# A transformer layer in fp32 by split matmuls: signs of two weight sums turned, two sums made in one VectorE operation, and a third made by an adding transfer that GpSimd issues

## Chip, cores, metric

The kernel runs on one core of a Trainium2 chip. The metric is device microseconds of one execution, as the median of several runs. Lower is better.

## The reference, cut to what matters

One layer of a hybrid decoder on 256 tokens of width 2048, all in float32:

```
xn   = rms_norm(h);  proj = xn @ w_in          # DeltaNet heads and attention heads
h    = h + concat(o_gdn, o_moba) @ w_o
hn   = rms_norm(h)
h    = h + (silu(hn @ w_gate) * (hn @ w_up)) @ w_down      # inner width 5632
gate = sigmoid(rms_norm(h) @ w_ple_gate)
h    = h + gate * (p @ w_ple_proj)
```

The change is in the last three lines: in the products with `w_gate` and `w_up`, with `w_down`, and with `w_ple_gate`.

## The kernel before

**Units.** A unit is 256 rows by 512 columns of a weight, held as `raw[j]`, 128 partitions x 2 x 512 float32 (512 KB). SyncE's queue (SP) loads it with one transfer into a ring of four buffers. ScalarE rounds it (`w_hi`), VectorE takes the remainder (`w_lo`, in `split`), and TensorE computes each product in three matmuls of 512 columns: hi by hi, hi by lo, lo by hi. A plain unit costs TensorE 12 matmuls. ScalarE and VectorE work three units ahead of TensorE (`LEAD = 3`). The load of unit u waits until `split` of unit u-4 is done (`lo_ready`), since it takes that buffer. ScalarE's rounding of unit u waits until TensorE has used unit u-4.

**Mixed units.** For some pairs of units the 2x2 block product is formed from seven products in place of eight (Winograd's form of Strassen), 21 matmuls for two units in place of 24. In a gate/up block of 16 units the pairs are (4, 5), (7, 8) and (10, 11) (`MIXED`, `SEQ`); the first block has its own order `FIRST_SEQ`, with pairs (5, 6), (8, 9) and (11, 12). There are 11 such blocks: 6 and 5, each group followed by a `down` stage of two halves with two pairs per half. The stage of the last gate (`PG_SEQ`) has pairs (6, 7) and (11, 12). That makes 43 pairs. In a pair, g is the first unit and u the second, each with two rows of 512 columns, 0 and 1. VectorE makes four weight sums in `split_mixed`:

```
t3 = u1 - u0          (L1913)
t1 = u0 - g0          (L1915, written over u0 in raw)
t2 = u1 - t1          (L1917)
t4 = g1 - t2          (L1919)
```

Then it splits unit u (whose first row is now t1), lets ScalarE round t3 alone (L1447) and t2 and t4 together (L1451), and takes the remainders t_lo (L1924 for t3, L1926 for t2 and t4). ScalarE rounds unit u (L1444) after t1 is there. TensorE (`mixed_units`) uses g, then u, then t3, then t2 and t4.

**What follows the sums.** SP's load four units after g waits for t4 (`t4_ready`), because t4 reads g's buffer; all later loads stand behind it in SP's order. In a loop block the load of unit 8 waits so for the sums of pair (4, 5), and that of unit 11 for the sums of pair (7, 8). In each loop block ScalarE and VectorE also turn the last block's activations between the parts of the first pair (`turned`, L1437 and L1903).

**GpSimd** makes masks at the start and small powers during the first half. In the stretch of the change it had two tasks, each of two tiny operations (`rstd`, L565 and L567): the inverse root of the mean square of h, once in the first gate/up block and once before the last gate.

Of the kernel before, what the change touches and what calls it, by code (L numbers as in the profile page):

```python
# [30 lines left out]
P = 128  # L31
# [182 lines left out]
def build(nc, A):  # L214
    FIRST, AT, BANK_OF = plan()

    with ExitStack() as ctx:
# [37 lines left out]
        for c in range(2):  # L255
# [40 lines left out]
        t3_raw = sb("t3_raw", [P, CB], at=mix + 62 * KIB)  # L296
# [15 lines left out]
        t24_raw = sb("t24_raw", [P, 2, CB], at=triu_at)  # L312
# [8 lines left out]
        assert triu_at + 4 * KIB <= place[0]  # L321
        rows = sb("rows", [NROW - KT, P])
        gains = sb("gains", [P, NROW + 2])
        G_ATTN, G_FFN, G_PLE, G_GDN, G_Q, G_K = 0, KT, 2 * KT, 3 * KT, 3 * KT + 1, 3 * KT + 2
        G_QS, G_OG = NROW, NROW + 1
# [4 lines left out]
        sc = {n: sb(n, [P, NT, HEADS]) for n in ("beta", "dt_in", "dt_abs", "dt_exp", "dt_ln", "dt_sum", "g", "gc", "egc")}  # L330
        ba_s = sb("ba_s", [P, NT, 2 * HEADS])
        ba_parts = sb("ba_parts", [P, NT, 4 * HEADS])
        warm = sb("warm", [P, 1])
# [54 lines left out]
        t1_ready, t2_ready, t3_ready, t4_ready = (sem(f"t{n}_ready") for n in (1, 2, 3, 4))  # L388
        t3_hi_ready, t24_hi_ready, t3_lo_ready, t24_lo_ready, t_used = (
            sem(n) for n in ("t3_hi_ready", "t24_hi_ready", "t3_lo_ready", "t24_lo_ready", "t_used"))  # L390
# [68 lines left out]
        def _(sp):  # L459
# [42 lines left out]
            for u0, u1, n, at, mg, md in ((U_GUA, U_DA, FF_A, 0, MIX_GUA, MIX_DA), (U_GUB, U_DB, FF_B, FF_A, MIX_GUB, MIX_DB)):  # L502
                def gate_up(i, seq):

                    for j, (side, g) in enumerate(seq):
                        w = w_gate if side == "gate" else w_up
                        if j >= RING and seq[j - RING] in [("gate", m) for m in MIXED]:
                            sp.wait_ge(t4_ready, i * len(MIXED) + (mg + MIXED.index(seq[j - RING][1]) + 1))
                            fetch(j, w, KU * g, i * CB + at * CB)
                        else:  # L510
                            load(i * (2 * UPB) + (u0 + j), j, w, KU * g, i * CB + at * CB)

                gate_up(0, SEQ if at else FIRST_SEQ)
                with sp.Fori(1, n) as i:
                    gate_up(i, SEQ)
                seq, dm, _ = down_order(n)
                with sp.Fori(0, 2) as i:
                    for j, (side, g) in enumerate(seq):
                        k, col = at * 4 + KU * g, i * (2 * CB) + side * CB
                        if j >= RING and seq[j - RING] in [(0, m) for m in dm]:  # L520
                            sp.wait_ge(t4_ready, i * 2 + (md + dm.index(seq[j - RING][1]) + 1))
                            fetch(j, w_down, k, col)
                        else:
                            load(i * len(seq) + (u1 + j), j, w_down, k, col)
            for b in range(4):
                load(U_PP + b, b, w_pp, 0, b * CB)
            for j, (side, g) in enumerate(PG_SEQ):
                if j >= RING and PG_SEQ[j - RING] in [(0, m) for m in PG_MIXED]:
                    sp.wait_ge(t4_ready, MIX_PG + PG_MIXED.index(PG_SEQ[j - RING][1]) + 1)
# [15 lines left out]
        def _(pool):  # L545
# [91 lines left out]
            for i in range(2):  # L637
                pool.wait_ge(h_sum, i + 1)
                rstd(h_rs[i][:], h_ms[i][:], h_s[i][:], 1.0 / D, EPS, h_rstd, i)


        @block.tensor
        def _(pe):
# [295 lines left out]
            def mixed_units(u, j, q, n):  # L939

                first, last = q == 0, q == len(MIXED) - 1
                g, a0, a1 = MIXED[q], slice(0, P), slice(P, TOK)
                k0, k1 = KU * g, KU * g + 1
                gh, gl = w_hi[j % RING], w_lo[j % RING]
                uh, ul = w_hi[(j + 1) % RING], w_lo[(j + 1) % RING]
                use(u)
                product(bg[0][:], xT_hi[:, k0, a0], xT_lo[:, k0, a0], gh[:, 0, :], gl[:, 0, :], first, last)
                product(pair[0][0][:], xT_hi[:, k1, a0], xT_lo[:, k1, a0], gh[:, 1, :], gl[:, 1, :], False,
                        last).then_inc(unit_used, 1)
                use(u + 1)  # L950
# [3 lines left out]
                pe.wait_ge(t3_lo_ready, n)  # L954
                product(bg[2][:], F_hi[:, q, 2, :], F_lo[:, q, 2, :], t_hi[:, 2, :], t_lo[:, 2, :], first, last)
                pe.wait_ge(t24_lo_ready, n)
                product(bg[1][:], F_hi[:, q, 0, :], F_lo[:, q, 0, :], t_hi[:, 0, :], t_lo[:, 0, :], first, last)
                product(pair[0][1][:], xT_hi[:, k1, a1], xT_lo[:, k1, a1], t_hi[:, 1, :], t_lo[:, 1, :], False,
                        last).then_inc(t_used, 1)
# [48 lines left out]
            def down(ud, bd, n, n0, m0, turn_last):  # L1008
# [3 lines left out]
                for m in range(2):  # L1012
                    c = m + (2 if n0 else 0)
                    for j, (side, g) in enumerate(seq):
# [7 lines left out]
                        if g in dm:  # L1022
# [25 lines left out]
                            pe.wait_ge(t3_lo_ready, count)  # L1048
                            product(bg[2][:], D_hi[:, q, 2, :], D_lo[:, q, 2, :], t_hi[:, 2, :], t_lo[:, 2, :], first, last)
                            pe.wait_ge(t24_lo_ready, count)  # L1050
                            product(bg[1][:], D_hi[:, q, 0, :], D_lo[:, q, 0, :], t_hi[:, 0, :], t_lo[:, 0, :], first, last)
                            product(pair[0][1][:], actT_hi[:, k1, a1], actT_lo[:, k1, a1], t_hi[:, 1, :], t_lo[:, 1, :], False,
# [32 lines left out]
            for j, (side, g) in enumerate(PG_SEQ):  # L1085
# [4 lines left out]
                if g in PG_MIXED:  # L1090
# [18 lines left out]
                    pe.wait_ge(t3_lo_ready, MIX_PG + q + 1)  # L1109
                    product(bg[2][:], E_hi[:, q, 3, :], E_lo[:, q, 3, :], t_hi[:, 2, :], t_lo[:, 2, :], first, last)  # L1110
                    pe.wait_ge(t24_lo_ready, MIX_PG + q + 1)
                    product(bg[1][:], E_hi[:, q, 1, :], E_lo[:, q, 1, :], t_hi[:, 0, :], t_lo[:, 0, :], first, last)
                    product(pair[0][1][:], xT_hi[:, k1, a1], xT_lo[:, k1, a1], t_hi[:, 1, :], t_lo[:, 1, :], False,
# [38 lines left out]
        def _(act):  # L1152
# [424 lines left out]
        def _(dve):  # L1577
# [328 lines left out]
            def split_mixed(u, j, n, first, between):  # L1906
# [45 lines left out]
            def add(o, a, b, done, count=None):  # L1952
# [3 lines left out]
                v.tensor_tensor(o, a, b, ALU.add).then_inc(done, 1)  # L1956

            def down(ud, n, n0, m0):

                seq, dm, end = down_order(n)  # L1960
                for j in range(2 * len(seq)):
# [15 lines left out]
                    if jj == end:  # L1977
# [3 lines left out]
                        add(v_s[:], bg[1][:], v_s[:], down_sum)  # L1981
                        add(u_s[:], bg[2][:], v_s[:], down_sum, d0 + 2)
                    if jj == end + 1:
                        add(o10, o10, u_s[:], down_sum, d0 + 3)
# [11 lines left out]
            def gate_up(i, u0, b0, n0, peeled, m0):  # L1996
                seq = FIRST_SEQ if peeled and n0 == 0 else SEQ
                mixed_end = seq.index(("up", MIXED[-1]))
                for j in range(2 * UPB):
# [15 lines left out]
                    if j == mixed_end:  # L2015
                        p1 = act_s[1]
                        dve.wait_ge(p1_copied, i + (n0 + (2 if n0 else 0) + 1))
                        v.tensor_tensor(v_s[:], bg[1][:], p1[:], ALU.add).then_inc(v_ready, 1)
# [4 lines left out]
                        v.tensor_tensor(gate_s[1][:], pair[0][1][:], u_s[:], ALU.add).then_inc(gate_sum, 1)  # L2023
# [29 lines left out]
            for u in range(U_PP, UNITS):  # L2053
# [12 lines left out]
                if u == U_PG + PG_END:  # L2066
                    dve.wait_ge(p1_copied, done + 4 + 1)
                    v.tensor_tensor(v_s[:], bg[1][:], act_s[1][:], ALU.add).then_inc(v_ready, 1)
# [4 lines left out]
                    v.tensor_tensor(gate_s[1][:], pair[0][1][:], u_s[:], ALU.add).then_inc(gate_sum, 1)  # L2073
# [36 lines left out]
```

## Time and profile before

| | |
|---|---|
| time, median of 3 runs | 1308.66 us (1308.38 to 1309.03) |
| span of the profiled execution | 1306.8 us |
| profiled execution's own time beside its span | not listed apart; the median is 1.9 us above the span |
| TensorE busy | 1299.9 us of the span |
| VectorE busy | 1041.3 us |
| ScalarE busy | 710.7 us |
| GpSimd busy | 57.2 us |
| read from HBM | 235.36 MB |

The span runs from the first to the last instruction. Matmuls are pipelined, so one that shows as 0.39 us long starts 0.23 us after the one before it. Idle time of an engine other than the one that sets the pace costs nothing by itself.

### The profile page before, as it was taken

The page shows a single profiled execution, that of the slowest core. Times are in us where ns is not written, and L with a number is a line of the kernel's source. Part 1 is how long each engine was busy: PE and PEld are TensorE (multiplying, and loading weights), DVE is VectorE, ACT ScalarE, POOL GpSimd, SP SyncE. Part 2 cuts the span into 40 slices and gives each one's busy share as a digit, 9 for nine tenths or more (in the row PEclk, how much of TensorE's full clock was granted, in tenths as well). Part 3 has the DMA queues.
Part 4 walks back from the last instruction along what each step waited for, and adds up shares of the span by engine and source line. Part 5 has one row for each costly group of instructions (what it writes and reads, how often), then busy time and mean ns, then how long its engine had stood idle before and what let it go on. Part 6 is the DMA issues. An engine that isn't in the chain of part 4 may idle for free.

```text
span 1306.8 us, 18407 instructions
## 1 busy us (share of the span) xinstructions
PE 1299.9 (99%) x6589; PEld 1074.1 (82%) x6589; DVE 1041.3 (80%) x1409; ACT 710.7 (54%) x946; POOL 57.2 (4%) x71
## 2 busy tenths in 40 slices
PE   9999999999999999999999999999999999999998
PEld 8788888888888888888888888888888888888887
DVE  6578885788586668999888978679888987968784
ACT  6576444544455556655555654445555555555653
POOL 5003000221000000000000000000000000000000
PEclk9999999999999999999999999999999999999999
DMA  8555554455444555665566656566666566556554
GB/s 272 178 176 162 160 147 129 146 147 148 145 127 145 178 176 161 215 219 181 188 198 205 204 187 215 182 211 188 195 205 214 181 189 210 190 178 224 178 179 163
DMA packets 126204, 238.37 MB, mean 182 GB/s; under 512 B 9711, under 2 KB 10786, under 8 KB 126138
## 3 DMA queue, kind: packets, MB, share of 16 engines
q1 hardware_dynamic: 126106, 237.48, 58.2%
q8 instruction: 42, 0.69, 0.2%
q14 instruction: 24, 0.20, 0.0%
q10 hardware_dynamic: 32, 0.01, 0.0%
HBM read 235.36 MB, written 2.10 MB: 182 GB/s over the span
## 4 chain that ended last, share of the span: by engine, by line
PE 97%; DVE 2%; ACT 0%; DMA 0%; issue 0%; DVEq 0%; ACTq 0%
PE pair L654 15%; PE pair L656 15%; PE pair L655 15%; PE pair L935 12%; PE pair L937 12%; PE pair L936 12%; PE bg L935 2%; PE bg L936 2%; PE bg L937 2%; PE bg L775 2%; PE bg L845 2%; PE bg L712 1%; PE bg L930 1%; DVE w_lo L1583 1%; PE bg L826 0%; PE bg L687 0%
## 5 line engine op out<-in xcount | busy, mean ns | idle before, releaser
L1583 DVE TENSOR_TENSOR w_lo<-raw,w_hi 128x1024 fp32r<-128x1024 f32 x442 | 533.1, 1222 | 160.7 <-ACT w_hi L1163 158.8
L1163 ACT ACTIVATE w_hi<-raw 128x1024 fp32r<-128x1024 f32 x399 | 416.4, 1056 | 254.6 <-PE pair L656 117.0
L654 PE MATMUL pair<-w_hi,xT_hi 128*128 128x512 f32 x716 | 289.7, 405 | 0.0
L656 PE MATMUL pair<-w_hi,xT_lo 128*128 128x512 f32 x716 | 279.9, 391 | 0.0
L655 PE MATMUL pair<-w_lo,xT_hi 128*128 128x512 f32 x716 | 279.4, 390 | 0.0
L656 PEld LDWEIGHTS pair<-w_hi,xT_lo 128*128 128x128 f32 x716 | 134.5, 188 | 29.1
L654 PEld LDWEIGHTS pair<-w_hi,xT_hi 128*128 128x128 f32 x716 | 134.7, 188 | 26.7 <-DVE w_lo L1583 0.3
L655 PEld LDWEIGHTS pair<-w_lo,xT_hi 128*128 128x128 f32 x716 | 134.9, 188 | 24.7
L1444 ACT ACTIVATE w_hi<-raw 128x1024 fp32r<-128x1024 f32 x43 | 45.7, 1063 | 141.5 <-DVE raw L1915 140.0
L935 PE MATMUL pair<-w_hi,actT_hi 128*128 128x512 f32 x296 | 115.7, 391 | 0.0
L937 PE MATMUL pair<-w_hi,actT_lo 128*128 128x512 f32 x296 | 115.2, 389 | 0.0
L936 PE MATMUL pair<-w_lo,actT_hi 128*128 128x512 f32 x296 | 115.2, 389 | 0.0
L935 PE MATMUL pair<-w_hi,xT_hi 128*128 128x512 f32 x226 | 88.2, 390 | 0.9 <-DVE w_lo L1583 0.9
L936 PE MATMUL pair<-w_lo,xT_hi 128*128 128x512 f32 x226 | 87.9, 389 | 0.0
L937 PE MATMUL pair<-w_hi,xT_lo 128*128 128x512 f32 x226 | 87.9, 389 | 0.0
L937 PEld LDWEIGHTS pair<-w_hi,actT_lo 128*128 128x128 f32 x296 | 55.6, 188 | 11.6
L936 PEld LDWEIGHTS pair<-w_lo,actT_hi 128*128 128x128 f32 x296 | 55.6, 188 | 11.4
L935 PEld LDWEIGHTS pair<-w_hi,actT_hi 128*128 128x128 f32 x296 | 55.6, 188 | 11.3
L1926 DVE TENSOR_TENSOR t_lo<-t_raw,t_hi 128x1024 fp32r<-128x1024 f32 x43 | 52.4, 1218 | 0.0
L935 PEld LDWEIGHTS pair<-w_hi,xT_hi 128*128 128x128 f32 x226 | 42.4, 188 | 10.5 <-DVE w_lo L1583 1.8
L937 PEld LDWEIGHTS pair<-w_hi,xT_lo 128*128 128x128 f32 x226 | 42.4, 188 | 8.9
L936 PEld LDWEIGHTS pair<-w_lo,xT_hi 128*128 128x128 f32 x226 | 42.4, 188 | 8.7
(386 smaller groups left out, 1959.8 us busy)
## 6 DMA issues: line engine op xcount, KB each, us to landing
raw<-in_w_in_dram SPq DMA_DIRECT2D x112, 512.0 KB, 3.8
raw<-in_w_gate_dram SPq DMA_DIRECT2D x88, 512.0 KB, 4.4
raw<-in_w_up_dram SPq DMA_DIRECT2D x88, 512.0 KB, 4.4
raw<-in_w_down_dram SPq DMA_DIRECT2D x88, 512.0 KB, 4.8
raw<-in_w_o_dram SPq DMA_DIRECT2D x32, 512.0 KB, 4.4
raw<-in_w_ple_gate_dram SPq DMA_DIRECT2D x32, 512.0 KB, 4.8
raw<-in_w_ple_proj_dram SPq DMA_DIRECT2D x4, 512.0 KB, 4.3
h<-in_x_dram SPq DMA_DIRECT2D x3, 512.0 KB, 7.8
```

Of the source, the lines that this page charges most:

```text
L654: mm(banks[t][:], hi[:, ts], wh, start=first, stop=False)
L655: mm(banks[t][:], hi[:, ts], wl, start=False, stop=False)
L656: m = mm(banks[t][:], lo[:, ts], wh, start=False, stop=last)
L775: m = mm(out[r][rs, j, :], lhs, rhs, start=True, stop=True)
L845: last = mm(o, l, r, start=True, stop=True)
L935: mm(o, hi, wh, start=first, stop=False)
L936: mm(o, hi, wl, start=False, stop=False)
L937: return mm(o, lo, wh, start=False, stop=last)
L1163: f(w_hi[j % RING][:], raw[j % RING][:], ACT.Copy).then_inc(hi_ready, 1)
L1444: f(w_hi[j % RING][:], raw[j % RING][:], ACT.Copy).then_inc(hi_ready, 1)
L1583: v.tensor_tensor(w_lo[j % RING][:], raw[j % RING][:], w_hi[j % RING][:].bitcast(F32), ALU.subtract).then_inc(lo_ready, 1)
L1926: v.tensor_tensor(t_lo[:, 0:2, :], t24_raw[:], t_hi[:, 0:2, :].bitcast(F32), ALU.subtract).then_inc(t24_lo_ready, 1)
```

## The change

The sums of g enter with the other sign, so that what was subtracted is added and the results are subtracted where they were added:

```
t1 = u0 + g0                       (made by a transfer)
t2 = u1 - t1
t3, t4 = g + t2                    (one operation on 128 x 1024: g0 + t2 and g1 + t2)
```

The first sum is made by a transfer from GpSimd's queue that reads g's first row (128 x 512, 256 KB) and adds it to u's first row in place. GpSimd waits until both units have landed, then issues it; ScalarE's rounding of u and VectorE's t2 wait for its 16 completion counts. The three sums lie side by side in `t_raw`; they are rounded by one ScalarE operation and their remainders taken by one VectorE operation of 128 x 1536. TensorE waits once for all three. GpSimd's 43 transfers stand in program order with its two `rstd` tasks: the first task stands between the second and the third transfer of the first block, the second task ahead of both transfers of the last gate. In the loop blocks, ScalarE's part of `turned` now stands ahead of its rounding of the sums. No instruction of TensorE is added or removed.

```
-                v.tensor_tensor(t3_raw[:], raw[ju][:, 1, :], raw[ju][:, 0, :], ALU.subtract).then_inc(t3_ready, 1)
-                dve.wait_ge(t3_ready, n)
-                v.tensor_tensor(raw[ju][:, 0, :], raw[ju][:, 0, :], raw[jg][:, 0, :], ALU.subtract).then_inc(t1_ready, 1)
-                dve.wait_ge(t1_ready, n)
-                v.tensor_tensor(t24_raw[:, 0, :], raw[ju][:, 1, :], raw[ju][:, 0, :], ALU.subtract).then_inc(t2_ready, 1)
+                dve.wait_ge(t1_ready, n * 16)
+                v.tensor_tensor(t_raw[:, 0, :], raw[ju][:, 1, :], raw[ju][:, 0, :], ALU.subtract).then_inc(t2_ready, 1)
                 dve.wait_ge(t2_ready, n)
-                v.tensor_tensor(t24_raw[:, 1, :], raw[jg][:, 1, :], t24_raw[:, 0, :], ALU.subtract).then_inc(t4_ready, 1)
+                v.tensor_tensor(t_raw[:, 1:3, :], raw[jg][:], t_raw[:, 0:1, :].to_broadcast([P, 2, CB]),
+                                ALU.add).then_inc(t34_ready, 1)
                 split(u, j)
                 if between:
                     between()
-                dve.wait_ge(t3_hi_ready, n)
-                v.tensor_tensor(t_lo[:, 2, :], t3_raw[:], t_hi[:, 2, :].bitcast(F32), ALU.subtract).then_inc(t3_lo_ready, 1)
-                dve.wait_ge(t24_hi_ready, n)
-                v.tensor_tensor(t_lo[:, 0:2, :], t24_raw[:], t_hi[:, 0:2, :].bitcast(F32),
-                                ALU.subtract).then_inc(t24_lo_ready, 1)
+                dve.wait_ge(t_hi_ready, n)
+                v.tensor_tensor(t_lo[:], t_raw[:], t_hi[:].bitcast(F32), ALU.subtract).then_inc(t_lo_ready, 1)
...
+            def first_sum(u, j, n):
+                jg, ju = (j - 1) % RING, j % RING
+                pool.wait_ge(raw_landed[jg], (u - 1 - jg) * (16 // RING) + 16)
+                pool.wait_ge(raw_landed[ju], (u - ju) * (16 // RING) + 16)
+                g.dma_start(raw[ju][:, 0, :], raw[jg][:, 0, :], accum_op=ALU.add).then_inc(t1_ready, 16)
...
+                    first_sum(i * (2 * UPB) + (u0 + j), j, i * len(MIXED) + (m0 + q + 1))
+                    if normed and q == 1:
+                        norm(0)
...
+            norm(1)
+            for q, m in enumerate(PG_MIXED):
+                j = PG_SEQ.index((1, m))
+                first_sum(U_PG + j, j, MIX_PG + q + 1)
...
-                act.wait_ge(t1_ready, n)
+                act.wait_ge(t1_ready, n * 16)
                 act.wait_ge(unit_used, u - (RING - 1))
                 f(w_hi[j % RING][:], raw[j % RING][:], ACT.Copy).then_inc(hi_ready, 1)
+                if between:
+                    between()
                 if not n0_first:
                     act.wait_ge(t_used, n - 1)
-                f(t_hi[:, 2, :], t3_raw[:], ACT.Copy).then_inc(t3_hi_ready, 1)
-                if between:
-                    between()
-                act.wait_ge(t4_ready, n)
-                f(t_hi[:, 0:2, :], t24_raw[:], ACT.Copy).then_inc(t24_hi_ready, 1)
+                act.wait_ge(t34_ready, n)
+                f(t_hi[:], t_raw[:], ACT.Copy).then_inc(t_hi_ready, 1)
```

SP's waits on `t4_ready` become waits on `t34_ready`, with the same counts. The results' signs are turned back in operations that were there before, by `subtract` in place of `add`.

## Rows read from the trace of the kernel before

**Rows 1.** The page: busy time by engine.
```profile
PE 1299.9 (99%) x6589; PEld 1074.1 (82%) x6589; DVE 1041.3 (80%) x1409; ACT 710.7 (54%) x946; POOL 57.2 (4%) x71
```

**Rows 2.** The page: the chain that ended last, shares by engine.
```profile
PE 97%; DVE 2%; ACT 0%; DMA 0%; issue 0%; DVEq 0%; ACTq 0%
```

**Rows 3.** Busy time by stretch: PE, PEld, DVE, ACT, POOL, clock, DMA share, GB/s.
```profile
600.00:700.00 100.00, 100.00 (x451) 82.96 (x450) 92.54 (x109) 56.45 (x65) 0.00 (x0) 1.00 0.63 197
```

**Rows 4.** First block, TensorE and VectorE: start, duration, instruction, idle before it.
```profile
522.90 0.50 PE L935 MATMUL pair<-w_hi,xT_hi 128*128 128x512 f32 x1 [0.61 <-DVE w_lo L1583]
...
531.02 0.50 PE L935 MATMUL pair<-w_hi,xT_hi 128*128 128x512 f32 x1 [0.30 <-DVE w_lo L1583]
...
532.51 0.39 PE L935 MATMUL bg<-t_hi,F_hi 128*128 128x512 f32 x1
...
518.84 0.69 DVE L1913 TENSOR_TENSOR t_raw<-raw 128x512 f32<-128x512 f32 x1
```

**Rows 5.** Groups by line: count, busy us, mean ns, idle before.
```profile
L1915 DVE TENSOR_TENSOR raw<-raw,raw 128x512 f32<-128x512 f32 x43 | 29.8, 692 | 1.5
...
L1926 DVE TENSOR_TENSOR t_lo<-t_raw,t_hi 128x1024 fp32r<-128x1024 f32 x43 | 52.4, 1218 | 0.0
...
L1451 ACT ACTIVATE t_hi<-t_raw 128x1024 fp32r<-128x1024 f32 x43 | 45.1, 1048 | 0.0
```

**Rows 6.** One loop block, VectorE and ScalarE in order of time.
```profile
633.42 0.69 DVE L1913 TENSOR_TENSOR t_raw<-raw 128x512 f32<-128x512 f32 x1
...
642.76 0.69 DVE L1913 TENSOR_TENSOR t_raw<-raw 128x512 f32<-128x512 f32 x1
...
650.81 0.69 DVE L1913 TENSOR_TENSOR t_raw<-raw 128x512 f32<-128x512 f32 x1
...
636.43 1.09 ACT L1437 ACTIVATE actT_hi<-bg 128x512 f32 x2
```

**Rows 7.** The same block, loads of units 5, 8, 11: issue, time to landing.
```profile
L468 SPq DMA_DIRECT2D raw<-in_w_up_dram x1: 373/373/373, 624.6 to 624.6; - x1
...
DMA to landing us min/median/max: 4.6/4.6/4.6
...
L468 SPq DMA_DIRECT2D raw<-in_w_up_dram x1: 373/373/373, 636.3 to 636.3; - x1
...
DMA to landing us min/median/max: 3.5/3.5/3.5
...
L468 SPq DMA_DIRECT2D raw<-in_w_up_dram x1: 372/372/372, 645.7 to 645.7; - x1
...
DMA to landing us min/median/max: 3.6/3.6/3.6
```

**Rows 8.** The same block, TensorE: first use of t_lo, pairs two and three.
```profile
649.49 0.39 PE L935 MATMUL bg<-t_hi,F_hi 128*128 128x512 f32 x1
...
656.97 0.39 PE L935 MATMUL bg<-t_hi,F_hi 128*128 128x512 f32 x1
```

**Rows 9.** Transfers by kind: KB each, us to landing.
```profile
out_dram<-h SPq DMA_DIRECT2D x1, 256.0 KB, 2.4
```

**Rows 10.** GpSimd's two small tasks in order of time.
```profile
524.75 1.09 POOL L565 TENSOR_SCALAR h_ms<-h_s 128x2 f32<-128x2 f32 x1 [137.64 <-DVE h_s L2014]
525.92 1.55 POOL L567 TENSOR_TENSOR h_rs<-h_ms,half 128x2 f32<-128x2 f32 x1
...
1228.00 0.62 POOL L565 TENSOR_SCALAR h_ms<-h_s 128x2 f32<-128x2 f32 x1 [700.52 <-DVE h_s L2064]
1228.70 1.15 POOL L567 TENSOR_TENSOR h_rs<-h_ms,half 128x2 f32<-128x2 f32 x1
```

**Rows 11.** Last gate, TensorE's first use of t_lo, pairs one and two.
```profile
1235.27 0.39 PE L935 MATMUL bg<-t_hi,E_hi 128*128 128x512 f32 x1
...
1248.19 0.39 PE L935 MATMUL bg<-t_hi,E_hi 128*128 128x512 f32 x1
```

**Rows 12.** Last gate, the load of unit 12, issued at 1234.8: time to landing.
```profile
DMA to landing us min/median/max: 5.2/5.2/5.2
```

More of the change, by code:

```diff
@@ L311, in build @@
         triu_at = place[0]
[L312 removed]
+        t_raw = sb("t_raw", [P, 3, CB], at=triu_at)
         triu = sb("triu", [P, P])
@@ L329, in build @@
         exp_a = sb("exp_a", [P, HEADS])
-        sc = {n: sb(n, [P, NT, HEADS]) for n in ("beta", "dt_in", "dt_abs", "dt_exp", "dt_ln", "dt_sum", "g", "gc", "egc")}
         ba_s = sb("ba_s", [P, NT, 2 * HEADS])
         ba_parts = sb("ba_parts", [P, NT, 4 * HEADS])
+        assert triu_at + 6 * KIB <= place[0]
+        gains = sb("gains", [P, NROW + 2])
+        G_ATTN, G_FFN, G_PLE, G_GDN, G_Q, G_K = 0, KT, 2 * KT, 3 * KT, 3 * KT + 1, 3 * KT + 2
+        G_QS, G_OG = NROW, NROW + 1
+        sc = {n: sb(n, [P, NT, HEADS]) for n in ("beta", "dt_in", "dt_abs", "dt_exp", "dt_ln", "dt_sum", "g", "gc", "egc")}
         warm = sb("warm", [P, 1])
@@ L636, in _, with norm, gate_up @@
                         post(*s)
-            for i in range(2):
+            def norm(i):
                 pool.wait_ge(h_sum, i + 1)
                 rstd(h_rs[i][:], h_ms[i][:], h_s[i][:], 1.0 / D, EPS, h_rstd, i)
+            def first_sum(u, j, n):
[3 more added lines that the diff above has]
+                g.dma_start(raw[ju][:, 0, :], raw[jg][:, 0, :], accum_op=ALU.add).then_inc(t1_ready, 16)
+            def gate_up(i, u0, m0, seq, normed):
+                for q, m in enumerate(MIXED):
+                    j = seq.index(("up", m))
+                    first_sum(i * (2 * UPB) + (u0 + j), j, i * len(MIXED) + (m0 + q + 1))
+                    if normed and q == 1:
+                        norm(0)
+            for n, n0, ug, ud, mg, md in ((FF_A, 0, U_GUA, U_DA, MIX_GUA, MIX_DA), (FF_B, FF_A, U_GUB, U_DB, MIX_GUB, MIX_DB)):
+                for i in range(n):
+                    gate_up(i, ug, mg, SEQ if n0 or i else FIRST_SEQ, not (n0 or i))
+                seq, dm, _ = down_order(n)
+                for m in range(2):
+                    for q, k in enumerate(dm):
+                        j = m * len(seq) + seq.index((1, k))
+                        first_sum(ud + j, j, md + 2 * m + q + 1)
+            norm(1)
+            for q, m in enumerate(PG_MIXED):
+                j = PG_SEQ.index((1, m))
+                first_sum(U_PG + j, j, MIX_PG + q + 1)
         @block.tensor
@@ L953, in mixed_units @@
                         False).then_inc(unit_used, 1)
-                pe.wait_ge(t3_lo_ready, n)
-                product(bg[2][:], F_hi[:, q, 2, :], F_lo[:, q, 2, :], t_hi[:, 2, :], t_lo[:, 2, :], first, last)
-                pe.wait_ge(t24_lo_ready, n)
+                pe.wait_ge(t_lo_ready, n)
+                product(bg[2][:], F_hi[:, q, 2, :], F_lo[:, q, 2, :], t_hi[:, 1, :], t_lo[:, 1, :], first, last)
                 product(bg[1][:], F_hi[:, q, 0, :], F_lo[:, q, 0, :], t_hi[:, 0, :], t_lo[:, 0, :], first, last)
-                product(pair[0][1][:], xT_hi[:, k1, a1], xT_lo[:, k1, a1], t_hi[:, 1, :], t_lo[:, 1, :], False,
+                product(pair[0][1][:], xT_hi[:, k1, a1], xT_lo[:, k1, a1], t_hi[:, 2, :], t_lo[:, 2, :], False,
                         last).then_inc(t_used, 1)
@@ L1108, in _ @@
                             False).then_inc(unit_used, 1)
-                    pe.wait_ge(t3_lo_ready, MIX_PG + q + 1)
-                    product(bg[2][:], E_hi[:, q, 3, :], E_lo[:, q, 3, :], t_hi[:, 2, :], t_lo[:, 2, :], first, last)
-                    pe.wait_ge(t24_lo_ready, MIX_PG + q + 1)
+                    pe.wait_ge(t_lo_ready, MIX_PG + q + 1)
+                    product(bg[2][:], E_hi[:, q, 3, :], E_lo[:, q, 3, :], t_hi[:, 1, :], t_lo[:, 1, :], first, last)
                     product(bg[1][:], E_hi[:, q, 1, :], E_lo[:, q, 1, :], t_hi[:, 0, :], t_lo[:, 0, :], first, last)
-                    product(pair[0][1][:], xT_hi[:, k1, a1], xT_lo[:, k1, a1], t_hi[:, 1, :], t_lo[:, 1, :], False,
+                    product(pair[0][1][:], xT_hi[:, k1, a1], xT_lo[:, k1, a1], t_hi[:, 2, :], t_lo[:, 2, :], False,
                             last).then_inc(t_used, 1)
@@ L1950, in turned_forms, with add @@
                                 ALU.subtract).then_inc(ff_free[q], 1)
-            def add(o, a, b, done, count=None):
+            def add(o, a, b, done, count=None, op=ALU.add):
                 if count:
                     dve.wait_ge(down_sum, count)
-                v.tensor_tensor(o, a, b, ALU.add).then_inc(done, 1)
+                v.tensor_tensor(o, a, b, op).then_inc(done, 1)
             def down(ud, n, n0, m0):
@@ L2022, in gate_up @@
                         dve.wait_ge(v_ready, i * 2 + (2 * n0 + 2))
-                        v.tensor_tensor(gate_s[1][:], pair[0][1][:], u_s[:], ALU.add).then_inc(gate_sum, 1)
+                        v.tensor_tensor(gate_s[1][:], pair[0][1][:], u_s[:], ALU.subtract).then_inc(gate_sum, 1)
                     if j == 2 * UPB - 1:
@@ L2067, in _ @@
                     dve.wait_ge(p1_copied, done + 4 + 1)
-                    v.tensor_tensor(v_s[:], bg[1][:], act_s[1][:], ALU.add).then_inc(v_ready, 1)
+                    v.tensor_tensor(v_s[:], bg[1][:], act_s[1][:], ALU.subtract).then_inc(v_ready, 1)
                     v.tensor_tensor(gate_s[0][:], pair[0][0][:], act_s[1][:], ALU.add).then_inc(gate_sum, 1)
@@ L2072, in _ @@
                     dve.wait_ge(v_ready, 2 * done + 2)
-                    v.tensor_tensor(gate_s[1][:], pair[0][1][:], u_s[:], ALU.add).then_inc(gate_sum, 1)
+                    v.tensor_tensor(gate_s[1][:], pair[0][1][:], u_s[:], ALU.subtract).then_inc(gate_sum, 1)
                     v.tensor_tensor(v_s[:], bg[3][:], v_s[:], ALU.add).then_inc(pg_parts, 1)
```

29 lines of the change are left out of this document (11 added, 18 removed).

## The prediction, made before the changed kernel was run

> **What bounds the kernel now.** I read the page's busy times first: TensorE is busy for 1299.9 of 1306.8 us, VectorE for 1041.3 [rows 1]. Then the chain that ended last: 97% of it is TensorE, 2% VectorE [rows 2]. So a shorter VectorE can give back only what TensorE loses to it. The places where it does are in the first gate/up block, where two matmuls waited for a remainder [rows 4]. In step, matmuls start 0.23 us apart; the one at 522.90 was due at 522.13 and the one at 531.02 at 530.56. That is 0.77 + 0.46 = 1.23 us, and it is all that the change can gain there. The table by stretch says what to fear instead: in the loop blocks VectorE is busy 92.5 of 100 us while TensorE has no gap [rows 3]. The two run close together, so a new delay ahead of VectorE may reach TensorE.
>
> **The change part by part.**
>
> *VectorE.* Per pair the four sums (4 x 0.69) and two remainders become one sum of 512 columns, one of 1024 and one remainder of 1536 [rows 5]. A 1024 operation takes 1.22, so 512 more columns add 0.53: the remainder of 1536 takes 1.75. VectorE saves about 1.0 us per pair, 43 us in all. Outside the first block this work is hidden behind TensorE, so I put its worth at nothing beyond the 1.23 us.
>
> *ScalarE.* One rounding of 1536 columns, about 1.5 us (1.05 for 1024, half as much again [rows 5]), starts only when both sums of the second operation are there. From the start of t2 the new order of a pair is: t2 and the double sum ready at +2.0 (0.73 from start to start, 1.22, a signal), rounding until +3.5, remainder until +5.3. Before, the last remainder ended at about +5.7 from the start of t3 (from 650.81) [rows 5, 6], which was VectorE's first sum.
>
> *The transfer, S.* From the landing of unit u to the moment when ScalarE and VectorE may go on, there is now one transfer of 256 KB within SBUF that reads two sources. No such operation is in the trace. From below, a plain store of 256 KB late in the kernel, from SP's queue, took 2.4 us from issue to landing [rows 9]; the sum reads the destination as well, is issued by GpSimd, whose smallest operations take 0.6 to 1.5 us [rows 10], and shares engines that are 63% busy [rows 3]. From above, the slowest load shown, twice the bytes and beside others, took 5.2 [rows 12]. I take S = 4.0: 2.4, plus 1.0 for GpSimd, plus 0.6 for the second read and the sharing; it is an estimate from these rows, between the two bounds.
>
> By the Trainium skill (DMA: Bandwidth & Descriptors, Anatomy of one DMA) a transfer issued from GpSimd takes about 2.0 us plus its bytes at 436 GB/s, which gives an estimate of 2.6 us for 256 KB; with it the total below would be 1314.3. The rows show no transfer from GpSimd, so the trace neither agrees nor differs; that case is the quick rival below.
>
> *One loop block with S = 4.0.* Pair (4, 5): unit 5's load is issued at 624.6 and lands after 4.6 [rows 7], its sum at 633.2; VectorE comes to the pair at 633.4 [rows 6], so no wait. The double sum is ready at 635.4 and SP issues the load of unit 8, 0.9 us earlier than before (636.3). ScalarE now first turns the activations, at 636.43 to 637.5 [rows 6], and rounds the three sums until 639.05; the remainder ends at 640.8, two splits follow (2.3), and VectorE is free for the second pair at 643.1, no earlier than before (642.76). Unit 8 lands 3.5 after issue, at 638.9; its sum at 642.9. Still no wait. The double sum is ready at 645.1, unit 11 lands 3.6 later at 648.7 [rows 7], and its sum is there at 652.7. VectorE would be free at 643.1 + 7.6 = 650.7 (5.2 for the pair, 2.3 for two splits), so here it waits 2.0. The remainder ends at 652.7 + 5.3 = 658.0. TensorE first uses it at 656.97 [rows 8]: it stalls 1.0 us. The second pair's remainder, at 648.4, is in time (649.49). TensorE sets the pace of the block, so the stall is not won back.
> As a rule: S - 2.95 per block from S = 2.95 to 4.2. Above 4.2 the first two pairs are late too, three transfers stand in one chain, and the stall is 3S - 11.4. With 10 blocks (the first of the second group has the same order): 10.5 us.
>
> *The down stages.* Their pairs lie four units apart with no turning between them; one hop has more cover. I put them at nothing up to S = 4; late, they would cost 2S - 7.7 twice by the same steps, 0.3 us each at 4.0 and 2.3 at 5.0. Small; left out of the sum.
>
> *The first block.* GpSimd's first small task now stands ahead of the third sum. It takes 2.7 us (524.75 to 527.47 [rows 10]) and starts when VectorE has done the second pair. VectorE came to that pair at 518.84 [rows 4] and will at about 518.4; its remainder ends 5.3 later, the mean square goes out at 523.8, the task ends at 526.6, the third sum lands at 526.6 + S, its remainder 5.3 later at 535.9. TensorE used it at 532.51 [rows 4], without the two waits at 531.28. Stall 4.6, less the 1.23 won: S - 0.6 = 3.4 us net.
>
> *The last gate.* The second small task stands ahead of the first sum there. It ends at 1229.85 [rows 10], though unit 7 has long landed. First sum at 1233.9, remainder at 1239.2, where TensorE wants it at 1235.27 [rows 11]: stall S - 0.07. The second pair: its load waits for the split after the first pair, at 1229.9 + S + 6.4, lands after 5.2 [rows 12], taken as 5.0; the sum takes S again, the remainder 5.3. That ends at 1246.6 + 2S = 1254.6 against 1248.19 [rows 11]. Stall in all 2S - 1.6 = 6.4 us. VectorE's cover does not help, for here the transfers wait for GpSimd and for the load.
>
> *Sum.* 10.5 + 3.4 + 6.4 = 20.3 us on the span of 1306.8: 1327.1. The median stood 1.9 above the span, so 1329.
>
> **Rivals.**
> *A quick transfer, S below 3.* The loop blocks have no stall, and the two fixed places remain: at 2.4, 1.8 + 3.2 = 5.0, time 1313.7. For it speaks the store of 2.4 us [rows 9]; against it, that this is a store with nothing else moving, from a queue other than GpSimd's.
> *Not slower.* GpSimd's small tasks lose their effect if S is 1.6 or less: then the last gate costs 1.6 and the first block 1.0, in all 2.6, about what can be told from no change; time 1311. At 1.0 it is 0.9 + 0.4 = 1.3 us, time 1310. It is decided by the one number S at the place of the second task. Against it: below every transfer of the rows. Faster by over 0.2% would take more than the 1.23 us that VectorE costs TensorE now.
> *A slow transfer, S of 5 or more.* Three transfers and two loads stand in one chain in each loop block: at 5.0 the blocks cost 36, the down stages 4.6, the first block 4.4, the last gate 8.4, together 53, time 1362. For it: VectorE is busy 92.5% [rows 3], and GpSimd's two operations took 1.09 and 1.55 in the first task but 0.62 and 1.15 in the second [rows 10], as if something held them; each pair's transfer also runs beside a load issued 1.1 us after the pair's own.
> The Trainium skill warns of this (SBUF — State Buffer, Who interferes with whom): GpSimd's writing of descriptors is blocked while VectorE runs an operation that holds both port pairs, but a sum of two SBUF tensors takes only the read side, so by the page this kernel's VectorE would not delay the transfer, and the time would be the first sum's; no row before shows which.
>
> **How the numbers follow.** S from 3 to 4.6, the forecast: 0.52. Quick, 1.7 to 3: 0.20, slower by a little. Slow, above 4.6: 0.18. Not slower: 0.10, of which 0.05 faster for gains that I don't see. With S at 1.9, under the store's 2.4, the two fixed places cost 3.5 and the time is 1312; at 5.0 it is 1362. The range 1311 to 1362 leaves out some 2 in 10. A measurement here tells about 0.2%, 2.6 us, from no change. Faster 0.05; the same 0.11 (the rest of that rival and part of the quick one); slower 0.84.
>
> **What would show it.** In the profile after, the 43 transfers should land about 4 us after issue. TensorE's waits should stand at the third pair of each loop block, about 1 us each, at the third pair of the first block and at both pairs of the last gate, all released by VectorE's t_lo or by the split, and VectorE before them by the transfer. VectorE's busy time should fall by about 43 us to 998, ScalarE's by about 7. If TensorE waits nowhere in the loop blocks, S was under 3. If it also runs through the last gate, the small task was not in the way. If waits stand at the second pair already, S was over 4.2. The prediction is wrong if S is outside 3 to 4.6, or if the loads become slower beside the transfers.

## The result and the profile after

The change made the kernel slower: 1399.09 us median (1396.62 to 1402.63) against 1308.76 measured beside it, a ratio of 1.069 [1.0676, 1.0708]. The forecast was 1329, the range 1311 to 1362. The profiled execution spans 1400.9 us, 94.1 more than before.

First the page after, busy time by engine and the chain that ended last, against [rows 1, 2].

```profile
PE 1332.5 (95%) x6589; PEld 1086.2 (78%) x6589; DVE 1005.3 (72%) x1280; ACT 708.7 (51%) x903; POOL 93.1 (7%) x114
...
PE 63%; DMA 18%; DVE 11%; ACT 4%; issue 3%; POOL 0%; DVEq 0%; ACTq 0%; POOLq 0%; SPq 0%
```

VectorE lost 36 us of busy time and TensorE, with the same 6589 matmuls, gained 32.6. TensorE's idle time, span less busy, went from 6.9 to 68.4. So 94.1 = 61.5 of idle time + 32.6 of longer busy time: two amounts to explain, not one. The chain, 97% TensorE before, now is 63% TensorE and 18% DMA.

TensorE's waits in the kernel after: who waited for whom, us in total, times, longest (`pair` and `bg` are what its matmuls write).

```profile
PE pair L962 <- DVE w_lo L1606: 36.2, 13, 3.8
PE bg L962 <- DVE w_lo L1606: 16.9, 8, 3.7
PE bg L962 <- DVE t_lo L1945: 5.7, 11, 0.6
PE bg L962 <- DVE actT_lo L1926: 2.7, 1, 2.7
```

VectorE is named, but VectorE itself waited. The groups of the kernel after say for what (count, busy us, mean ns, idle before and its releaser); the last row is GpSimd's transfer.

```profile
L1468 ACT ACTIVATE w_hi<-raw 128x1024 fp32r<-128x1024 f32 x43 | 45.6, 1060 | 185.4 <-DMA raw<-raw 179.1
...
L1937 DVE TENSOR_TENSOR t_raw<-raw 128x512 f32<-128x512 f32 x43 | 29.8, 692 | 114.3 <-DMA raw<-raw 112.2
L645 POOL DMA_DIRECT2D raw<-raw x43 | 37.2, 866 | 843.8 <-DMA raw<-in_w_up_dram 590.0
```

One loop block shows how: its three transfers, and the load of unit 13 (duration of the issue in ns, when; then time to landing).

```profile
L645 POOL DMA_DIRECT2D raw<-raw x3: 859/859/862, 649.1 to 668.9; - x3
...
DMA to landing us min/median/max: 3.4/3.6/7.0
...
L466 SPq DMA_DIRECT2D raw<-in_w_up_dram x1: 372/372/372, 669.1 to 669.1; - x1
...
DMA to landing us min/median/max: 7.0/7.0/7.0
```

The first two transfers took 3.6 and 3.4. The third, issued at 668.88 with a load 0.25 behind it, took 7.0, and so did that load. The same block in order of time: VectorE's second sum, then TensorE.

```profile
675.90 0.69 DVE L1937 TENSOR_TENSOR t_raw<-raw 128x512 f32<-128x512 f32 x1 [5.66 <-DMA raw<-raw]
...
674.83 0.39 PE L964 MATMUL pair<-w_hi,xT_lo 128*128 128x512 f32 x1
679.04 0.79 PE L962 MATMUL pair<-w_hi,xT_hi 128*128 128x512 f32 x1 [3.83 <-DVE w_lo L1606]
679.63 0.63 PE L963 MATMUL pair<-w_lo,xT_hi 128*128 128x512 f32 x1
```

After the wait matmuls are 0.42 to 0.6 us apart instead of 0.23. The table by stretch tells why (PE busy with matmuls, granted clock, DMA share, GB/s).

```profile
670.00:675.00 5.00, 5.00 (x24) 1.00 0.73 156
675.00:679.00 4.00, 0.21 (x1) 0.96 0.06 6
679.00:680.00 1.00, 0.96 (x2) 0.50 0.76 176
680.00:681.00 1.00, 1.00 (x4) 0.50 0.95 358
681.00:682.00 1.00, 1.00 (x4) 0.50 0.91 295
682.00:683.00 1.00, 1.00 (x5) 0.97 0.48 182
683.00:685.00 2.00, 2.00 (x11) 1.00 0.69 170
```

TensorE was idle from 675.2 to 679.0; for the next 3 us the granted clock was 0.50, the lower of its two levels (1.2 GHz). Of the 17 waits of over 2 us in the stretch of the change 14 were followed by such a stretch at 0.50, none of the shorter ones was by itself. In five of the 14 it began before the wait ended, by up to 1.2 us. The last row of the same table over all 14 stretches:

```profile
sum 54.59, PE 50.74; mean PE 3.62
```

TensorE was busy for 50.7 us at 0.50, and at half the rate some 25 of them are loss, 1.8 us for each of the 14. Most of the other 7 us are no slower work: a matmul shows as 0.39 us long but the next one starts after 0.23, so the first 0.16 of a wait counts as busy, 5.3 us for the 33 waits of the lines above.

Over all 43 transfers the split is sharp. Nineteen had a load issued between 1.0 us before and 0.55 after them; they took 5.3 to 7.0 us, median 6.2. Twenty-four had none: 3.2 to 4.3, median 3.4. The third pair of every loop block is of the first kind, and so are six of the eight of the down stages.

### The profile page after: what moved, and what is told of

The parts are those of the page before. It is cut to its first block, busy times and chain, and to the rows that moved or that the text cites. A ratio compares the mean times of both kernels' runs of the same rounds, so it can differ in the third digit from the quotient of the medians.

```text
span 1400.9 us, 18364 instructions
## 1 busy us (share of the span) xinstructions
PE 1332.5 (95%) x6589; PEld 1086.2 (78%) x6589; DVE 1005.3 (72%) x1280; ACT 708.7 (51%) x903; POOL 93.1 (7%) x114
## 4 chain that ended last, share of the span: by engine, by line
PE 63%; DMA 18%; DVE 11%; ACT 4%; issue 3%; POOL 0%; DVEq 0%; ACTq 0%; POOLq 0%; SPq 0%
PE pair L681 12%; PE pair L683 11%; PE pair L682 11%; DMA raw<-raw 10%; PE pair L962 6%; PE pair L963 6%; PE pair L964 6%; DMA raw<-in_w_up_dram 5%; DVE w_lo L1606 4%; DVE t_raw L1939 3%; ACT t_hi L1474 2%; DMA raw<-in_w_down_dram 2%; DVE t_raw L1937 2%; PE bg L802 2%; PE bg L872 1%
## 5 line engine op out<-in xcount | busy, mean ns | idle before, releaser
L683 PEld LDWEIGHTS pair<-w_hi,xT_lo 128*128 128x128 f32 x716 | 134.4, 188 | 29.1
L682 PEld LDWEIGHTS pair<-w_lo,xT_hi 128*128 128x128 f32 x716 | 134.8, 188 | 24.7
L1937 DVE TENSOR_TENSOR t_raw<-raw 128x512 f32<-128x512 f32 x43 | 29.8, 692 | 114.3 <-DMA raw<-raw 112.2
L645 POOL DMA_DIRECT2D raw<-raw x43 | 37.2, 866 | 843.8 <-DMA raw<-in_w_up_dram 590.0
L1945 DVE TENSOR_TENSOR t_lo<-t_raw,t_hi 128x1536 fp32r<-128x1536 f32 x43 | 75.6, 1758 | 19.6 <-ACT t_hi L1474 19.6
L1474 ACT ACTIVATE t_hi<-t_raw 128x1536 fp32r<-128x1536 f32 x43 | 63.9, 1487 | 38.7 <-DVE t_raw L1939 38.7
```

The source lines that it names most:

```text
L682: mm(banks[t][:], hi[:, ts], wl, start=False, stop=False)
L683: m = mm(banks[t][:], lo[:, ts], wh, start=False, stop=last)
L1474: f(t_hi[:], t_raw[:], ACT.Copy).then_inc(t_hi_ready, 1)
L1937: v.tensor_tensor(t_raw[:, 0, :], raw[ju][:, 1, :], raw[ju][:, 0, :], ALU.subtract).then_inc(t2_ready, 1)
L1945: v.tensor_tensor(t_lo[:], t_raw[:], t_hi[:].bitcast(F32), ALU.subtract).then_inc(t_lo_ready, 1)
```

## Experiments

The first four were to decide between three theories. **A**: the loss is the wait for the transfer, 3.5 us alone and 6 to 7 beside a load, with slow matmuls behind it. **B**: the transfers' traffic slows TensorE's weight loads. **C**: one wait for three sums, with the turning of the activations ahead of their rounding, makes the remainders late.

**e1: VectorE makes the first sum, no transfer.** All else as in the kernel after.

```
-  g.dma_start(raw[ju][:, 0, :], raw[jg][:, 0, :], accum_op=ALU.add).then_inc(t1_ready, 16)
...
+  v.tensor_tensor(raw[ju][:, 0, :], raw[ju][:, 0, :], raw[jg][:, 0, :], ALU.add).then_inc(t1_ready, 1)
```

> The changed kernel with the first sum made by VectorE again (added, 128 x 512) and no transfer from GpSimd; the turned signs, the double sum, the one rounding and the one remainder stay. Theory A (the loss is the wait for the transfer): 1306 to 1309 us, at most the 1.23 us that VectorE cost TensorE before are won. Theory B (the transfers' traffic slows the weight loads): the same, since the traffic is gone. Theory C (one wait for all three sums, and turning the activations ahead of their rounding, makes the remainders late): 1330 us or more, TensorE waiting for t_lo in each loop block.

1317.15 us, ratio 1.0063 [1.0049, 1.0076]. So 82 of the 90 us go with the transfer; 8.4 stay, which A did not expect and C had far too large. In nine of the ten loop blocks TensorE now waits 0.39 to 0.43 for the third pair's remainder, in the first block three times 0.6 and in a down stage once 0.5. One such place of e1, VectorE's remainder and TensorE's wait for it:

```profile
659.02 1.76 DVE L1921 TENSOR_TENSOR t_lo<-t_raw,t_hi 128x1536 fp32r<-128x1536 f32 x1 [0.48 <-ACT t_hi L1449]
...
660.84 0.50 PE L937 MATMUL bg<-t_hi,F_hi 128*128 128x512 f32 x1 [0.43 <-DVE t_lo L1921]
```

**e2: e1 with 43 transfers that nobody waits for** (192 KB each, a buffer added onto itself, at the places of the real ones).

```
+  g.dma_start(idle_b[:], idle_b[:], accum_op=ALU.add).then_inc(idle_done, 16)
```

> As the kernel before this one, with VectorE's own first sum, and beside it GpSimd issues 43 adding transfers at the same points, of 192 KB within a buffer that nothing reads. Theory A: within 3 us of the kernel without them, 1306 to 1312 us; the transfers themselves land after 3 to 7 us. Theory B: 1350 us or more, weight loads landing later by over 1 us. Theory C: as the kernel without them.

1317.17 us, ratio 1.0067 [1.0051, 1.0082]: e1's time, though these transfers took 2.9 to 6.4 us themselves. The loads of gate, up and down weights landed after 4.1, 4.4 and 4.7 us in the median, against 4.0, 4.4 and 4.6 in e1. B falls: the traffic, here three quarters of the bytes, costs nothing that shows; the waiting does.

**e3: the load of unit 13 held in the loop blocks until the third sum has landed and VectorE has used it.**

```
+  elif seq is SEQ and j == 13:
+      sp.wait_ge(t2_ready, i * len(MIXED) + (mg + 3))
+      fetch(j, w, KU * g, i * CB + at * CB)
```

> The changed kernel, but in the ten gate/up blocks after the first SP issues the load of unit 13 only when VectorE has made t2 of the third pair (some 4 us later), so that no load starts beside the third transfer. Theory A (a transfer takes 3.5 us alone and 6 to 7 beside a load that starts with it): the third transfers fall from 5.8 to 7.0 us to about 3.5, TensorE's waits at the third pair from 2.5 to 3.8 us to under 1, and with the slow matmuls behind them 4 us per block are won: 1350 to 1365 us. Theory B or a slowness of the third transfer for another reason (its buffers, GpSimd): transfers stay at 6 us and the time within 10 us of 1399, or longer, since a load was put off.

1360.36 us, ratio 1.039 [1.0374, 1.0406]: 38.7 less than the kernel after for a load that starts later. The third transfers of the loop blocks fell to 3.3 to 3.8, here that of the block shown above:

```profile
L648 POOL DMA_DIRECT2D raw<-raw x1: 862/862/862, 659.9 to 659.9; - x1
...
DMA to landing us min/median/max: 3.3/3.3/3.3
```

The waits for w_lo behind them are gone in seven of the ten blocks and at most 0.9 in the others, and one of 0.6 for t_lo stands in each. That is A.

**e4: GpSimd's two small tasks behind the sums that they preceded.**

```
-  if normed and q == 1:                 # first block
+  if normed and q == 2:
...
-  norm(1)                               # last gate: ahead of both sums
...
+  if q == 0:                            # behind the first sum
+      norm(1)
```

> The changed kernel with GpSimd's two small tasks put behind the transfer that they stood ahead of (the first behind the third sum of the first block, the second behind the first sum of the last gate). If they delayed these sums, as the prediction had it: the first block wins 2 to 4 us, the last gate 2 to 3 us, time 1393 to 1396. If they were not in the way: 1399 within 2 us.

1378.62 us, ratio 1.0539 [1.0509, 1.0568]: 20 less, where I expected 3 to 6. Most of the gain is in the loop blocks, which the edit does not touch: there the load now came 0.48 to 0.62 us after the third transfer instead of 0.25 to 0.45, and the median of these transfers fell from 6.3 to 4.7. What moved the two apart by some 0.2 us was not settled. It led to e9.

**e5 and e6: which half of C.** Both start from e1. In e5 ScalarE turns the activations behind its rounding, as the kernel before did:

```
-  if between:
-      between()
...
   act.wait_ge(t34_ready, n)
   f(t_hi[:], t_raw[:], ACT.Copy).then_inc(t_hi_ready, 1)
+  if between:
+      between()
```

> The kernel after without its transfer (VectorE makes the first sum), and ScalarE turns the activations behind its rounding of the three sums again instead of ahead of it. The kernel with the first sum on VectorE took 1317.2, 8.4 over the kernel before, with a wait of TensorE of 0.4 us for the remainder of the third pair in each loop block. Theory T (the turning, about 1.1 us once in a block ahead of the first pair's rounding, delays a VectorE that works without a break up to the third pair): the wait goes, and the time is within 2 us of the kernel before, 1307 to 1311. Rival R (the one rounding of 1536 columns ends 0.4 to 0.5 later than VectorE is ready for it, in every pair): the wait stays in the loop blocks, 1314 to 1317.

In e6 the second sum is rounded as soon as it is there:

```
+  act.wait_ge(t2_ready, n)
+  f(t_hi[:, 0, :], t_raw[:, 0, :], ACT.Copy)
   act.wait_ge(t34_ready, n)
-  f(t_hi[:], t_raw[:], ACT.Copy).then_inc(t_hi_ready, 1)
+  f(t_hi[:, 1:3, :], t_raw[:, 1:3, :], ACT.Copy).then_inc(t_hi_ready, 1)
```

> The kernel after without its transfer (VectorE makes the first sum), and ScalarE rounds the second sum as soon as it is there and the third and fourth by an operation of 1024 columns, so that the last rounding ends some 0.4 us earlier; the turning stays ahead of it. Theory R (the late rounding): VectorE's waits of 0.48 us for the rounding go in every pair, TensorE's waits in the loop blocks with them, 1308 to 1312. Theory T (the turning): little changes, 1315 to 1318. If both count: between, 1311 to 1315.

e5 took 1322.65 us, ratio 1.0106 [1.0091, 1.0122], slower than e1 by 5.5: the turned activations come late now, and the wait for t_lo stays. Two rows of e5, one block:

```profile
600.60 0.49 PE L937 MATMUL bg<-w_hi,xT_hi 128*128 128x512 f32 x1 [0.40 <-DVE actT_lo L1901]
...
618.91 0.50 PE L937 MATMUL bg<-t_hi,F_hi 128*128 128x512 f32 x1 [0.32 <-DVE t_lo L1921]
```

e6 took 1309.19 us, ratio 1.0002 [0.9993, 1.0011]: the kernel before again, with TensorE busy as before:

```profile
PE 1300.9 (99%) x6589; PEld 1074.2 (82%) x6589; DVE 1035.5 (79%) x1323; ACT 714.7 (55%) x946; POOL 56.4 (4%) x71
```

So the whole 8 us was the one rounding of 1536 columns, which ends 0.48 after VectorE is ready for it. From the first sum's start to the remainder's end VectorE takes 5.75 us for a pair in the kernel before, 6.05 in e1 and 5.57 in e6 (medians of 43). The turned signs, the double sum, the one remainder and the turning ahead of the rounding together cost nothing and bring nothing.

**e7: ten extra matmuls ahead of the wait in the third pair** (into a bank that is free then; their result is not used).

```
+  for _ in range(fill if q == 2 else 0):
+      mm(bg[3][:], xT_hi[:, 0, a0], xT_hi[:, 0:2, :].rearrange("p k n -> p (k n)"), start=True, stop=True)
   use(u + 1)
...
+  mixed_units(u, j, q, i * len(MIXED) + (m0 + q + 1), 0 if peeled else 10)
```

> The kernel after with ten extra matmuls of 512 columns (2.3 us, their result is not used) ahead of TensorE's wait in the third pair of the eight loop blocks that are not the first of their group. Theory: TensorE stood idle there for 2.5 to 3.8 us, and the granted clock then was 0.50 for 3 us, in which it did half of its work; with the idle time mostly filled the clock stays at 1.00, and each block gains about 1.5 us, 1399 - 12 = 1387 (1383 to 1391). Rival (the matmuls after the wait are slow because their operands come late or because the transfers take memory bandwidth): the same 1397 to 1403, or later by what the extra matmuls add where a wait is shorter than 2.3.

1392.57 us, ratio 1.0634 [1.0618, 1.065], some 6.5 less with 90 matmuls more (they stand in nine blocks, not in the eight that I counted). The profiled executions tell more. 90 x 0.227 = 20.4 us of matmuls were added; TensorE's busy time without them is 1343.5 - 20.4 = 1323.1, 9.4 less than after, and idle time with them is 48.4 + 20.4 = 68.8, as after. So the wait is the same and the matmuls behind it are faster. The same place of the block in e7:

```profile
675.00:676.00 1.00, 1.00 (x6) 1.00 0.00 0
676.00:677.00 1.00, 0.68 (x3) 1.00 0.33 39
677.00:678.00 1.00, 1.00 (x6) 1.00 0.77 240
```

The clock stays at 1.00, here and in all nine filled blocks; in the kernel after it had fallen in seven of them. The gain, 1.0 us per block, is two thirds of what I expected; a shorter wait of 0.57 for t_lo came up in most of these blocks, which had been hidden behind the slow matmuls.

**e8: half the columns, 128 KB** (half of the first sum is left out).

```
-  g.dma_start(raw[ju][:, 0, :], raw[jg][:, 0, :], accum_op=ALU.add).then_inc(t1_ready, 16)
+  g.dma_start(raw[ju][:, 0, 0:CB // 2], raw[jg][:, 0, 0:CB // 2], accum_op=ALU.add).then_inc(t1_ready, 16)
```

> The kernel after with a transfer of half the columns, 128 KB instead of 256 (half of the first sum is left out). Theory F (most of a transfer's time does not depend on its bytes): 2.9 to 3.7 us alone and 4.7 to 6.5 beside a load, the time 1385 to 1400. Theory Y (it goes by the bytes): 2.0 to 2.5 us alone and 3 to 4 beside a load, with waits in the loop blocks under 1.5 us, the time 1330 to 1360.

1374.78 us in one run, between the two theories. Transfers without a load beside them took 2.6 to 3.7, median 2.7; the 19 others 4.2 to 6.0, median 5.1. Half the bytes save 0.7 us of 3.4, and 1.1 of 6.2 beside a load: most of the time does not go by bytes.

**e11: a copy in place of the add** (the first sum is left out).

```
-  g.dma_start(raw[ju][:, 0, :], raw[jg][:, 0, :], accum_op=ALU.add).then_inc(t1_ready, 16)
+  g.dma_start(raw[ju][:, 0, :], raw[jg][:, 0, :]).then_inc(t1_ready, 16)
```

> The kernel after with a transfer that copies the gate's columns over the up's instead of adding them (the add of the first sum is left out). Theory R (the read of the destination and the add cost about 0.6 us, as the prediction took it): 2.4 to 2.8 us alone against 3.2 to 3.5, 1375 to 1392. Rival N (the add is free, the time is GpSimd's issue and the bytes written): 3.1 to 3.5 alone, 1390 to 1405.

1352.47 us in one run, under both theories' times. Without a load beside them 2.2 to 3.5, median 2.4; with one 2.5 to 5.6, median 4.3. So the add costs 1.0 us, not 0.6, and part of it is in issuing: GpSimd's issue takes 0.54 us, not 0.86. GpSimd's transfers in e11, issue times in ns, then all of them to landing, and the share of that queue:

```profile
L645 POOL DMA_DIRECT2D raw<-raw x43: 536/536/788, 503.7 to 1282.8; - x43
...
DMA to landing us min/median/max: 2.2/3.1/5.6
...
q0 software_dynamic: 3440, 11.27, 2.3%
```

and the same lines of the kernel after:

```profile
L645 POOL DMA_DIRECT2D raw<-raw x43: 850/859/1090, 503.7 to 1333.0; - x43
...
DMA to landing us min/median/max: 3.2/4.0/7.0
...
q0 software_dynamic: 6192, 11.27, 4.6%
```

For the same bytes the adding transfer keeps the engines busy twice as long: 4.6% of 1400.9 over 43 is 1.5 us of all sixteen, against 0.7.

**e9: the load of unit 13 held only until GpSimd has issued the transfer and run a smallest operation.**

```
   g.dma_start(raw[ju][:, 0, :], raw[jg][:, 0, :], accum_op=ALU.add).then_inc(t1_ready, 16)
+  pool.wait_ge(lo_ready, u - 1)
+  g.memset(mark[:, n - 1:n], 0.0).then_inc(issued, 1)
...
+  elif seq is SEQ and j == 13:
+      sp.wait_ge(issued, i * len(MIXED) + (mg + 3))
+      fetch(j, w, KU * g, i * CB + at * CB)
```

> The kernel after, with the load that follows the third transfer of each loop block held until GpSimd has issued that transfer and then run a smallest operation: so it is issued some 1.0 us after the transfer instead of 0.25 to 0.45, and not only when the sum has landed. In the earlier runs a transfer with a load issued from 0.9 us before it to 0.45 after took 5.3 to 7.3 us, one with a load 0.5 to 0.6 after it 4.4 to 6.1, one with none within 0.7 some 3.2 to 4.9. Theory H (it is the order in which transfer and load are queued): the third transfers take 3.3 to 4.4, the loop blocks lose under 1.5 us each, the time 1355 to 1368, as with the load held to the end (1360.4). Rival W (any load moving beside a transfer slows it): 5 to 7 us still, 1385 to 1400.

1373.22 us, ratio 1.0494 [1.0478, 1.051]. The loads now start 0.99 to 1.00 after the transfers, and these take 3.7 to 4.1: H in what it says of the transfers. The time missed its range by 5, and lies 13 above e3: at 3.8 instead of 3.4 all ten blocks wait again for w_lo at the third pair, 0.3 to 1.2, beside the 0.6 for t_lo. The profiled executions of the two lie 9.0 apart; 4.7 of these are the waits for w_lo (6.4 in all against 1.7), 3.0 are TensorE's busy time, and the rest lies where the two kernels do not differ. The third transfers of the loop blocks in order: a load 0.25 to 0.45 behind, median 6.3 (the kernel after); 0.48 to 0.62, 4.7 (e4); 1.0, 3.8 (e9); none, 3.4 (e3).

**e10: all of it together.** The second load behind each pair held as in e9 in every gate/up and down stage, the small tasks as in e4, the rounding as in e6.

> The kernel after, with the second load behind each pair held in the same way in all gate/up and down stages, GpSimd's two small tasks behind the sums that they preceded, and the rounding in two operations (second sum, then third and fourth). It is the transfer with every cost taken away that the runs have named. If these are all: transfers of 3.2 to 4.4 us nearly everywhere, TensorE's waits under 1 us each, 1314 to 1328. If a cost is missing, or the held loads come late for the units behind them: 1330 or more. It is faster than the kernel before only if the wait for 3.3 us is covered in every pair, which I expect not.

1346.89 us, ratio 1.0295 [1.0281, 1.0309], the best of the kernels with the transfer and still 38 above the kernel before. My expectation was too low by 19. In the gate/up stages transfers took 3.2 to 4.3, as expected, but in the down stages 3.4 to 5.4 and in the last gate 5.5 and 3.8; and 3.7 to 4.3 in a third pair is not free. TensorE's waits in e10:

```profile
PE bg L973 <- DVE w_lo L1619: 11.9, 6, 2.5
PE pair L973 <- DVE w_lo L1619: 11.5, 11, 1.9
```

At the third pair the loop blocks wait 0.47 to 1.89, the down stages up to 2.5. Five transfers of the down stages took 4.4 to 5.4 although the load behind them came 1.13 after them, later than in e9; there the load ahead was issued 2.1 to 2.6 before the transfer, in the third pairs 2.8 to 3.2, and so was on its way longer beside it. No run tests whether that is the reason. Idle time is 31.3 us and TensorE's busy time 14 above before; 24.4 + 14 = 38.4 makes up the span's difference.

## Why the prediction was wrong, point by point

*What bounds the kernel*: right. VectorE's groups in the pairs fell from 201.0 to 158.1 us, 42.9 as predicted (its busy time on the page only by 36.0, to 1005.3 and not 998, and ScalarE's by 2, not 7: the page counts time once where two operations of an engine overlap, and the plain sums of durations fell by 43.4 and 8.1), and none of it came back as time. e6 keeps part of the saving and is at the kernel before.

*The transfer, S, the same for every pair*: this is the step that failed. The median of all 43 is 4.0, as predicted, but that is luck: only six lie between 3.6 and 4.4, and no pair can be costed with it. Alone S was 3.4, beside a load that starts with it 6.2, and 19 transfers took longer than the 5.2 that was to bound S from above. Of the 74 us by which the span missed the sum, 21 stand at the third pairs, 16 in the down stages and 33 in TensorE's busy time. The prediction had the clue, a load issued 1.1 us after each pair's own, and used it only as an argument for the slow rival; it did not look at which load stands within a microsecond of each transfer. The parts were off as well: the copy from GpSimd with its issue took 2.4, as the plain store from SP's queue did [rows 9], so the 1.0 allowed for GpSimd is not seen, and the add took 1.0, not 0.6. By the Trainium skill (DMA: Bandwidth & Descriptors, Queues, rings and completion order) each DMA engine takes turns, packet by packet, between the queues that it has work for. The trace agrees in that a transfer and a load issued 0.25 apart both took 7.0. That some 0.2 us more of a head start saves the transfer 1.6 only the runs show. The 2.6 us estimated by the Trainium skill's fit (DMA: Bandwidth & Descriptors, Anatomy of one DMA) lie between the measured copy, 2.4, and the add, 3.4.

*The loop blocks*: the formula held, its input did not. Only the third transfer was late, so S - 2.95 applies; with 6.3, 6.8, 7.0, 5.9 and 6.4 in the first group it gives 3.4, 3.9, 4.1, 3.0 and 3.5, and TensorE waited 2.5, 3.6, 3.8, 2.5 and 3.2. The third pairs of the ten blocks waited 31.5 us in all instead of 10.5. A second transfer beside a load added 1.2, and a first one 2.7, for the turned activations.

*A missing term*: a long wait of TensorE costs more than its length. Of the 32.6 us of longer busy time some 25 are matmuls at 0.50 of the clock, 1.8 for each of the 14 waits behind which it fell. e7 shows for nine blocks that the idle time does it: filled, 9.4 us of busy time came back. The sum had no such term.

*The down stages at nothing*: wrong. Six of their eight transfers stand beside a load, 5.6 to 7.0 us, and TensorE waited there 16.2 us, of which 0.4 to 0.6 at most pairs for t_lo. By the prediction's 2S - 7.7 at 6.3 it would have been 4.9 for each of the two stages, of the 10.0 and 6.2 measured.

*ScalarE's one rounding*: the chain was costed rightly (+5.3; the median of the 43 is 5.32, against 5.75 before), with VectorE's wait of 0.48 for the rounding in it. What was overlooked is that it pays only while the first sum is off VectorE: with that sum back, the rounding costs 8.0 us (e1 against e6). What it costs in the kernel after itself no run shows.

*The first block*: right as to GpSimd's task. The third transfer landed at 530.9 (forecast 530.6), and TensorE used its remainder at 536.4 (535.9). That the block lost 4.3 us of idle time, with the 0.9 of before off 3.4, as predicted, is in part luck: 3.3 stand at the third pair, and two waits of 0.4 and 0.6 took the place of the two that were to go. *The last gate*: near. Its waits are 3.8 us where 6.4 stood, but part of the loss is matmuls at 0.50 behind the first wait. From VectorE's last reduction ahead of GpSimd's task (1227.76 before, 1315.29 after) to TensorE's first use of the second t_lo it was 20.43 us before [rows 11] and 26.63 after, 6.2 more.

*The rivals*: the total is beyond the slow one's 1362, but not by its mechanism: no chain of three slow transfers (all but three of the first and second ones in a block took 3.2 to 4.3). The warning that VectorE might hold up GpSimd's writing of descriptors did not come true: GpSimd's issue took 0.85 to 0.89 us in 42 of the 43, 1.09 in the first, whether VectorE was at work beside it, as in most, or idle. That agrees with the exception of the Trainium skill (SBUF — State Buffer, Who interferes with whom) for sums of SBUF tensors. As for slower loads, the last sign that was named: beside a transfer loads took up to 7.4 us, 6.3 at most in these stages before; in e2, where they took up to 6.5, no time was lost by it.

## What to carry to other kernels

A transfer placed between a landing and the next use has to be priced together with the loads that the same events release: look in the trace for every load issued from a microsecond before it to half a microsecond behind it, and cost it nearly twice as long there (6.2 against 3.4 us here). An adding transfer between SBUF buffers costs 3.4 us of waiting to save a VectorE operation of 0.69, so it needs a pair that waits elsewhere for longer than that. Merging operations makes the first result as late as the last, and an idle stretch of TensorE is to be costed with the slow matmuls behind it.

## What had not been expected of the hardware

The adding transfer keeps the DMA engines busy twice as long as a copy of the same bytes (1.5 us against 0.7) and takes GpSimd 0.86 us to issue against 0.54. In the third pairs a head start of 1.0 us over a load instead of 0.25 to 0.45 decides between 3.8 and 6.3 us for a transfer. After 14 of 17 waits of 2.1 to 3.8 us TensorE was granted 0.50 of its clock, mostly for some 3 us; after two, at 966.57 and 1109.43, for 5 us and more, and after waits of 2.60, 3.08 and 2.32 (at 1062.77, 1158.08 and 1270.24) not at all. In other runs shorter waits were followed by it too, 1.75 us in e4 and 1.91 in e10. What sets these apart stays open.
